# Down projections of a decoder trunk as one Strassen step, with weight sums built in device memory

## The reference

```
def swiglu(x, w_gu, w_down):
    g, u = jnp.split(x @ w_gu, 2, axis=-1)
    return (jax.nn.silu(g) * u) @ w_down
...
    for l in range(DEPTH):
        x = layer_norm(ALPHA * x + 0.5 * swiglu(x, ffn1_w_gu[l], ffn1_w_down[l]), ln_w[l, 0], ln_b[l, 0])
        mix = hybrid_mixer(x, positions, w_in[l], b_in[l], attn_sinks[l], mlstm_norm_w[l],
                           conv_w[l], w_branch[l], w_out[l])
        x = layer_norm(ALPHA * x + mix, ln_w[l, 1], ln_b[l, 1])
        x = layer_norm(ALPHA * x + 0.5 * swiglu(x, ffn2_w_gu[l], ffn2_w_down[l]), ln_w[l, 2], ln_b[l, 2])
```

## Time and profile before

| what | value |
|---|---|
| median of three runs | 2335.39 us |
| profiled execution: its own time | 2335.44 us |
| profiled execution: its span | 2333.7 us |
| PE busy, share of the span | 2319.9 us, 99% |
| DVE busy | 1565.4 us, 67% |
| ACT busy | 971.3 us, 42% |
| POOL busy | 19.0 us, 1% |
| mean DMA rate over the span | 106 GB/s |
| first down stage, 233.4 to about 353 us: DVE busy in its first 60 us | 28.02 us |
| gate and up stage, 33 to 133 us: DVE busy | 91.69 us |

### The profile page before, as it was taken

How to read it: one execution, slowest core, us unless ns; L and a number is a source line. 1 busy time by engine, 2 the same in 40 slices (tenths; PEclk the granted TensorE clock), 3 DMA queues, 4 the chain that set the end, 5 groups by cost and what they waited for, 6 DMA issues and landing times.

```text
span 2333.7 us, 34884 instructions
## 1 busy us (share of the span) xinstructions
PE 2319.9 (99%) x14416; PEld 2089.5 (90%) x14416; DVE 1565.4 (67%) x2262; ACT 971.3 (42%) x1497; POOL 19.0 (1%) x16
## 2 busy tenths in 40 slices
PE   8999999999999999999999999999999999999998
PEld 8999888888888899998899998898888888999987
DVE  8988446554654698883598883565455647988834
ACT  5444324434443354443254453233344433544531
POOL 0000300000000000000000000000000000000000
PEclk9999999999999999999999999999999999999999
DMA  5333434323233333333233333243233233333421
GB/s 166 106 101 118 141 104 136 95 73 96 94 95 108 127 91 109 108 110 109 90 92 109 109 109 108 88 152 97 73 95 99 83 117 114 104 102 99 131 104 72
DMA packets 295053, 247.08 MB, mean 106 GB/s; under 512 B 13136, under 2 KB 256880, under 8 KB 294896
## 3 DMA queue, kind: packets, MB, share of 16 engines
q1 hardware_dynamic: 294352, 244.34, 33.8%
q10 hardware_dynamic: 544, 0.52, 0.1%
HBM read 238.51 MB, written 6.31 MB: 105 GB/s over the span
## 4 chain that ended last, share of the span: by engine, by line
PE 99%; DVE 0%; DMA 0%; DVEq 0%; ACT 0%; issue 0%
PE main L1585 10%; PE main L1587 10%; PE main L1586 10%; PE main L1741 6%; PE main L1739 6%; PE side L1740 6%; PE side L1739 6%; PE main L1740 6%; PE side L1741 6%; PE main L1691 5%; PE main L1693 5%; PE main L1692 5%; PE side L1691 4%; PE side L1692 4%; PE side L1693 4%; PE main L1674 1%
## 5 line engine op out<-in xcount | busy, mean ns | idle before, releaser
L991 DVE TENSOR_TENSOR wl<-raw,wh 128x1024 fp32r<-128x1024 f32 (+2 forms) x277 | 305.9, 1147 | 447.6 <-ACT wh L649 447.3
L649 ACT ACTIVATE wh<-raw 128x1024 fp32r<-128x1024 f32 (+2 forms) x277 | 260.8, 994 | 319.1 <-PE side L1693 175.2
L1585 PE MATMUL main<-xh,wh 128*128 128x512 f32 x848 | 334.4, 394 | 0.0
L1587 PE MATMUL main<-xl,wh 128*128 128x512 f32 x848 | 330.4, 390 | 0.0
L1586 PE MATMUL main<-xh,wl 128*128 128x512 f32 x848 | 330.2, 389 | 0.0
L1587 PEld LDWEIGHTS main<-xl,wh 128*128 128x128 f32 x848 | 159.2, 188 | 33.7
L1585 PEld LDWEIGHTS main<-xh,wh 128*128 128x128 f32 x848 | 159.2, 188 | 33.2 <-issue 0.3
L736 ACT ACTIVATE wh<-tw 128x1024 fp32r<-128x1024 f32 x80 | 84.8, 1060 | 248.3 <-PE side L1741 117.4
L1586 PEld LDWEIGHTS main<-xh,wl 128*128 128x128 f32 x848 | 159.4, 188 | 31.7
L1739 PE MATMUL side<-sum_hi,wh 128*128 128x256 f32 x640 | 181.1, 283 | 0.0
L1740 PE MATMUL side<-sum_hi,wl 128*128 128x256 f32 x640 | 181.1, 283 | 0.0
(11 more groups left out here) (301 smaller groups left out, 5712.4 us busy)
## 6 DMA issues: line engine op xcount, KB each, us to landing
raw<-gu SPq DMA_DIRECT2D x326, 256.0 KB, 4.0
raw<-w_in SPq DMA_DIRECT2D x100, 512.0 KB, 4.6
raw<-down SPq DMA_DIRECT2D x80, 512.0 KB, 4.6
raw<-w_branch SPq DMA_DIRECT2D x24, 512.0 KB, 4.4
raw<-w_out SPq DMA_DIRECT2D x16, 512.0 KB, 4.4
raw<-w_in SPq DMA_DIRECT2D x28, 256.0 KB, 3.6
raw<-gu SPq DMA_DIRECT2D x13, 512.0 KB, 5.8
raw<-down SPq DMA_DIRECT2D x16, 256.0 KB, 2.7
```

The lines of the kernel that those rows point to most:

```text
L649: ins = act.activation(put(wh[block_of(g)]), get(raw[slot]), ACT.Copy)
L991: ins = V.tensor_tensor(put(wl[b]), get(raw[slot]), f32(put(wh[b])), ALU.subtract)
L1585: T.matmul(out, hi, rh(k), start=k == 0, stop=False)
L1587: ins = T.matmul(out, hi, rl(k), start=False, stop=k == kk - 1)
```

## The change

The hidden activations A (512 by 2816) and the down weight W (2816 by 1024) are each cut in two by two blocks: A by tokens (256 each) and by hidden chunks (11 each, `KH`), W by hidden chunks and by output columns (512 each). Seven block products replace eight. They run one after the other, each over all its 11 chunks, in the order P1, P5, P6, P3, P2, P7, P4. `DOWN` lists the 22 slabs of this: three slabs (4, 4 and 3 chunks) for each product, four (4, 3, 2 and 2) for P4. A product has two token tiles, so it takes 11 x 2 x 3 = 66 matmuls.

- The token operands are `hp` itself for P1, P2 and P4, and sums made by DVE (`operand_sum`) for the others, in `sf` (laid over `xh`) or in place in `hp`. ACT and DVE split each into `ah` and `al`, one buffer of four for each slab.
- The weight operands of P5, P6, P7 and P4 are the sums T1 to T4 of blocks of W. They lie in device memory (`tsum`). POOL builds them with DMAs: for each sum and each quarter of its rows first a copy (`begin`) and then a DMA that adds onto it, 32 DMAs of 352 rows by 512 columns (0.72 MB) for each of the four down stages. They are started when `w_lo` reaches 8, the first 32 before `angles`, the other 96 after it. SP waits for a sum (`blocks_summed`) before it loads its first slab.
- The results go from PSUM into `xt` product by product (`residual`), where P6, P7 and P4 collect on top of P1 in the same two banks, and P3 on top of P5. A product that reuses a bank waits in PE until DVE has read it (`part_used`).
- The order of the tails is written anew: tiles 0 and 1 are complete after P2 and are normalised by DVE while it prepares P4's first two slabs, tiles 2 and 3 after P4. The load of `xt` in the first block moves from the down stage to the gate and up stage (`c == 12`).

```diff
-S_FFN = KF + 12
+KH = KF // 2
+P1, P5, P6, P3, P2, P7, P4 = range(7)
+DOWN = tuple((r, k, n) for r in range(6) for k, n in ((0, 4), (4, 4), (8, 3))) + tuple((P4, k, n) for k, n in ((0, 4), (4, 3), (7, 2), (9, 2)))
+ENDS = tuple(max(j for j, d in enumerate(DOWN) if d[0] == r) for r in range(7))
+SUMMED = tuple(j for j, d in enumerate(DOWN) if d[0] in (P5, P6, P3, P7))
+T1, T2, T3, T4 = range(4)
+TURNED_BLOCKS = {P5: T1, P6: T2, P7: T3, P4: T4}
+PARTS = 4
+PART = KH * P // PARTS
+S_FFN = KF + len(DOWN)
...
+        sf = at("sf", [P, KH, 256], F32, xh_at)
...
+        ah = [big(f"ah{i}", kb, [P, 4, 256], F32R) for i, kb in enumerate((60, 44, 52, 76.25))]
+        al = [big(f"al{i}", kb + 4, [P, 4, 256], F32R) for i, kb in enumerate((60, 44, 52, 76.25))]
...
+        tsum = [nc.dram_tensor(f"tsum{i}", (4, KH * P, HALF), F32, kind="Internal").ap() for i in range(2 * DEPTH)]
...
+                return (r_, p_, q_)[(n - KF) % 3]
...
+                    if c == 12 and layer + f == 0:
+                        for t in range(NB):
+                            sp.dma_start(xt[:, t, :], token_tile(x_in, t)).then_inc(xt_in[t].sem, 16)
+                for j, (r, k0, kk) in enumerate(DOWN):
+                    if r in TURNED_BLOCKS:
+                        if k0 == 0:
+                            for i in range(PARTS):
+                                sp.wait_ge(blocks_summed[i].sem, 16 * (8 * u + 2 * TURNED_BLOCKS[r] + 2))
+                        src = tsum[u][TURNED_BLOCKS[r]].rearrange("(k p) n -> p k n", p=P)[:, k0:k0 + kk, :]
+                    else:
+                        low_rows, right = {P1: (0, 0), P2: (KH, 0), P3: (KH, HALF)}[r]
+                        src = wd[:, low_rows + k0:low_rows + k0 + kk, right:right + HALF]
+                    load(n0 + KF + j, src)
+                    if j == 4:
+                        sp.wait_ge(hid_f.sem, hid_f.val(layer, 22 * f + 22))
+                        rows(layer, 2 * f)
+                        if layer == 0 and f == 0:
+                            sp.dma_start(positions_in[:, :], positions[0, :].partition_broadcast(P)).then_inc(pos_in.sem, 16)
...
-            def hidden_high(layer, f, c):
-                act.wait_ge(hid_f.sem, hid_f.val(layer, 22 * f + c + 1))
-                act.activation(hh[c][:, :], hp[:, c, :], ACT.Copy).then_inc(*o.up(hid_h))
+            def operand_high(layer, f, j):
...
+                if j == 0:
+                    act.wait_ge(w_lo.sem, 2 * (n0 + KF))
+                else:
+                    act.wait_ge(slab_done.sem, n0 + KF + max(0, j - 3))
+                if j in SUMMED:
+                    act.wait_ge(tokens_summed.sem, len(SUMMED) * (2 * layer + f) + SUMMED.index(j) + 1)
+                else:
+                    act.wait_ge(hid_f.sem, hid_f.val(layer, 22 * f + (k0 + kk if r == P1 else KF)))
+                act.activation(ah[j % 4][:, 0:kk, :], operand(j), ACT.Copy).then_inc(*o.up(part_hi))
...
+                for j in range(2, len(DOWN)):
+                    split(n0 + KF + j)
+                    operand_high(layer, f, j)
+                    if layer == 0 and f == 0 and j == 14:
...
+                    if j == 17:
+                        root(L, 0)
+                    if j == 18:
+                        root(L, 1)
...
+            def sum_blocks_of(layer, f):
...
+                for t in (T1, T2, T3, T4):
+                    for i, t_, out_, begin, add in steps:
+                        if t_ == t:
+                            if 8 * u + 2 * t:
+                                pool.wait_ge(blocks_summed[i].sem, 16 * (8 * u + 2 * t))
+                            G.dma_start(out_, begin).then_inc(blocks_summed[i].sem, 16)
+                    for i, t_, out_, begin, add in steps:
+                        if t_ == t:
+                            pool.wait_ge(blocks_summed[i].sem, 16 * (8 * u + 2 * t + 1))
+                            G.dma_start(out_, add, accum_op=ALU.add).then_inc(blocks_summed[i].sem, 16)
+            pool.wait_ge(w_lo.sem, 8)
+            sum_blocks_of(0, 0)
             angles()
+            for layer, f in ((0, 1), (1, 0), (1, 1)):
+                sum_blocks_of(layer, f)
...
-            def hidden_low(layer, f, c):
-                dve.wait_ge(hid_h.sem, hid_h.val(layer, 22 * f + c + 1))
-                V.tensor_tensor(hl[:, c, :], hp[:, c, :], f32(hh[c][:, :]), ALU.subtract).then_inc(*o.up(hid_l))
+            def operand_sum(layer, f, j):
...
+                a11, a21 = hp[:, k0:k0 + kk, 0:256], hp[:, k0:k0 + kk, 256:512]
+                a12, a22 = hp[:, KH + k0:KH + k0 + kk, 0:256], hp[:, KH + k0:KH + k0 + kk, 256:512]
+                held = sf[:, k0:k0 + kk, :]
+                if r == P5:
+                    dve.wait_ge(slab_done.sem, n0 + KF)
+                    dve.wait_ge(hid_f.sem, hid_f.val(layer, 22 * f + KF))
+                    out_, a, b, op = held, a21, a22, ALU.subtract
+                elif r == P6:
+                    dve.wait_ge(part_lo.sem, len(DOWN) * u + j - 2)
+                    out_, a, b, op = held, held, a11, ALU.subtract
+                elif r == P3:
+                    dve.wait_ge(part_lo.sem, len(DOWN) * u + j - 2)
+                    out_, a, b, op = held, a12, held, ALU.add
+                else:
+                    dve.wait_ge(tokens_summed.sem, len(SUMMED) * u + 3)
+                    out_, a, b, op = a21, a11, a21, ALU.subtract
+                V.tensor_tensor(out_, a, b, op).then_inc(*o.up(tokens_summed))
+            def operand_low(layer, f, j):
+                u, kk = 2 * layer + f, DOWN[j][2]
+                dve.wait_ge(part_hi.sem, len(DOWN) * u + j + 1)
+                V.tensor_tensor(al[j % 4][:, 0:kk, :], operand(j), f32(ah[j % 4][:, 0:kk, :]), ALU.subtract).then_inc(*o.up(part_lo))
...
+            def residual(layer, f, r):
...
+                for i in range(2):
+                    if i == 0:
+                        dve.wait_ge(part_done.sem, norm_parts(L) + r + 1)
+                    else:
+                        dve.wait_ge(slab_done.sem, n0 + KF + ENDS[r] + 1)
+                    t = i if r in (P1, P6, P3, P2) else 2 + i
+                    p = 1 if r in (P5, P6, P3, P7) else 0
+                    some = xt[:, t, HALF * p:HALF * p + HALF]
+                    ps = pm[2 + i][:, :] if r in (P1, P6, P7, P4) else sd[:, i, :] if r in (P5, P3) else pm[i][:, :]
+                    told = part_used if r != P4 else acc_free if i else None
+                    if r in (P1, P5, P6, P4):
+                        if L == 0 and r in (P1, P5):
+                            dve.wait_ge(xt_in[t].sem, 16)
+                        V.scalar_tensor_tensor(out=some, in0=some, scalar=ALPHA, in1=ps, op0=ALU.mult,
+                                               op1=ALU.subtract if r == P6 else ALU.add).then_inc(*o.up(told))
+                    else:
+                        dve.wait_ge(part_used.sem, 12 * u + 2 * {P3: P6, P2: P1, P7: P5}[r] + i + 1)
+                        V.scalar_tensor_tensor(out=some, in0=ps, scalar=-1.0 if r == P7 else 1.0, in1=some, op0=ALU.mult,
+                                               op1=ALU.add).then_inc(*o.up(told))
+                    if r in (P3, P2, P7, P4):
+                        o.settle()
+                        V.bn_stats(lst[:, t, p, :], some).then_inc(*o.up())
+                    if r in (P2, P4):
+                        o.settle()
+                        apart(dve)
+                        V.bn_aggr(lag[:, t, :], lst[:, t, :, :]).then_inc(*o.up(var_ready))
+                    if r == P4:
+                        scale(L, t)
+                        finish(L, t)
+                        if i == 0 and L < NORMS - 1:
+                            split(n0 + S_FFN + 1)
...
+                for j in range(2, len(DOWN)):
+                    if j in SUMMED:
+                        operand_sum(layer, f, j)
+                    split(n0 + KF + j)
+                    operand_low(layer, f, j)
+                    if j - 2 in ENDS:
+                        residual(layer, f, ENDS.index(j - 2))
+                    if j in (17, 18):
+                        if j == 17:
+                            dve.wait_ge(rows_in_.sem, 32 * (L + 1))
+                        scale(L, j - 17)
+                        finish(L, j - 17)
+                if L < NORMS - 1:
+                    low(L + 1, 0)
+                    low(L + 1, 1)
+                    split(n0 + S_FFN)
+                residual(layer, f, P4)
+                if L < NORMS - 1:
+                    low(L + 1, 2)
+                    if in_sums(n0 + S_FFN + 2):
+                        sums_13(n0 + S_FFN + 2)
+                    low(L + 1, 3)
...
-                pe.wait_ge(hid_f.sem, hid_f.val(layer, 22 * f + KF - 1))
-                to_tokens(3 * layer + 2 * f, n0 + KF, GROUPS_FFN, lambda k: hh[k], lambda k: hl[:, k, :],
-                          lambda k: pe.wait_ge(hid_l.sem, hid_l.val(layer, 22 * f + k + 1)))
...
+                def bank(r, i):
```

(103 more changed lines are left out.)

92 lines of the change are left out of this document (43 added, 49 removed).

## The result

Four runs after the change gave 2348.25 to 2355.91 us, median 2354.36, against 2335.31 before (2335.05 to 2335.64): ratio 1.0078, interval 1.0065 to 1.009. The kernel is 19 us slower. I had forecast 2310 and faster. The profiled execution took 2355.91, with a span of 2354.1.

A forecast was written before the change was run, and what follows sets the result against it. PE, busy 99% of the span, was taken to bound the kernel. 2335.4 - 59.9 (matmuls) + 16 (DVE idling) + 6 (hand-overs) + 12 (new DMAs and POOL's arithmetic) = 2309.5, say 2310; range 2286 to 2362.

The forecast's parts named there:

- PE's matmuls, -59.9: Down stages: 462 matmuls of the same shape, 0.2267 us apart, saving 15.0 us a stage, 59.9 in all.
- DVE's list, +16: Down stages: DVE's list equals PE's, so its idling delays P4's first matmul; 4 us a stage, 16 in all (0 to 36).
- Hand-overs, `xt` and POOL's arithmetic, +6, +2 and +5: Late tiles at stage ends 6 us; `xt`'s load in gate and up 2; DVE slowed beside the angles, first stage, 5.
- the bare saving: Whole kernel: the time before less only the removed matmuls, 2335.4 - 59.9, with no costs added.
- The adding DMAs, t = 5: POOL's sum DMAs: 5 us each (2.9 to 12.1), 160 us for a stage's 32, T1 complete near 90, hidden.
- That cover holds unless the landing doubles. I put 5 us: Gate and up stage: SP's loads, 9.5 us ahead and landing in some 4, lose 5 us to the DMAs (0 to 50).
- 1, DVE keeps up: Down stages: raw slabs land in time and DVE's list has no hole; 2287 us; chance 0.20.
- 2: First down stage: slow adding DMAs make ACT wait 32t - 237 for the angles, 2361 at t = 9; chance 0.14.
- its companion from the Trainium skill: DVE's two-port modes starve GpSimd's DMAs, so adds would crawl; by inference two-input subtraction does not, adding nothing.
- 3, the loads starve: Gate and up stage: loads queue behind 2 KB pieces, some 8 slabs pay 6 or 7 us; about 2355; chance 0.12.
- 4, DVE idles twice as much: Down stages: DVE idles 9 us a stage or more through handshakes and landings; 2330, nearly no gain; chance 0.14.
- The page's formula: POOL's DMAs: 2.0 us and bytes over 436 GB/s, 3.65 us for 0.72 MB, 117 us for 32 end to end.

The follow-up runs named there:

- e1: The changed kernel without POOL's sum DMAs; P5, P6, P7 and P4 read a plain block of the down weight, sums left out; 2309.28 us.
- e5: e1 with P7's update read out of PSUM ahead of slab 19's low parts, as in e3; 2283.61 us.
- e2: The changed kernel with `tsum`'s rows padded by 64 bytes, so copies from sum to sum move as 2 KB rows, not 45 KB pieces; 2333.85 us.
- e3: The changed kernel with P7 read out of PSUM right after slab 18's low parts, before slab 19's and tile 1's normalising; 2328.63 us.
- e4: The changed kernel with both the padded rows of e2 and the early reading of P7 of e3; 2309.62 us.
- e10: e7 without the padding of the sums' rows, so copies from sum to sum are again 45 KB pieces, one DMA in flight; 2299.93 us.
- e7: e4 with each of POOL's 128 DMAs issued only when the one before has landed; 2301.94 us.
- e6: e4 with POOL issuing the 96 DMAs of the later blocks' sums only when the first down stage is over; 2295.99 us.
- e11: e6 with one POOL DMA in flight, except T4's four adds, which wait only for their own copy; angles between T4's copies and adds; 2294.64 us.

## Why the prediction was wrong, point by point

- **PE's matmuls, -59.9: right.** In the second stage P1's first starts at 1086.70 and P7's last at 1176.26, 396 of them 0.2267 apart.
- **DVE's list, +16: right in place and cause, too small.** I had 88.0 us of work and 4 of idling; the window from 1088 to 1181 has 87.2 of DVE busy, and its waits for ACT there sum to 5.1. The gap is 4.6 to 5.0 where 4 was put. What I left out is the slow clock after it. Wait and clock together are 6.4 a stage by e1 and e5, 25.7 in all where 16 were put. The windows of the changed kernel:

```profile
1088.00:1181.00 93.00, 88.65 (x392) 73.06 (x390) 87.22 (x93) 55.32 (x64) 0.00 (x0) 0.99 0.59 193
```

- **Hand-overs, `xt` and POOL's arithmetic, +6, +2 and +5: too large together.** e5 has these and nothing else, and stands 2283.6 - 2275.5 = 8.1 above the bare saving, 13 less 4.9. That DVE slows by a quarter to a third beside the angles holds (1590 against 1223 ns).
- **The adding DMAs, t = 5: the price in sequence about right, each one dearer.** 32 of them took 180 us (45.8 to 226.2), 5.6 each, and SP hardly waited for a sum. But one lands in 8.2 and not in 5, and T1 was complete at 97.6, not near 90. My ground, "the four quarters overlap", holds for the copies only, two at a time in 2 KB pieces and four in long ones.
- **The step that failed: "That cover holds unless the landing doubles. I put 5 us".** The term measured 45.1 (e1). The landing of `raw<-gu` between 50 and 240 went from 3.9 (e1) to 6.8 in the middle, and at the bursts to over 16. It was also priced for the gate and up stage alone. The loads of the first down stage and of the mixer beside the same DMAs were put at nothing, and 16.5 and 11.2 of the 45 were lost there. I set the mean DMA share, 37%, against the mean cover, and took a DMA from device memory to itself to be made of 2 KB pieces strung out by waits. What decides is what stands in front of a load at one moment: three or four copies of 45 KB pieces. Of the 45.1 us the bursts are about 20: 20.5 from the changed kernel to e2 and 19.0 from e3 to e4, which differ in the padding alone. (e3 to e10 is 28.7, but its waits act on all of POOL's DMAs, and with short pieces the same waits gained 7.7, e4 to e7.) The next sums beside the first down stage, where loads are wanted soonest, are 13.6 (e4 to e6), and 12.4 stay (e6 to e5), whose place no run isolates. With so few runs, which spread by up to 20 us, these sizes are good to a few us.
- **The rivals.** 1, DVE keeps up (2287), is what e5 shows once the order is mended and the DMAs are gone: 2283.6. 2 did not come (SP and ACT did not wait for sums or angles), but e7 brought it about, at the price of its formula. Of its companion from the Trainium skill ("SBUF — State Buffer", "SBUF: two separate sides") the inference was the half that fits, that a two-input subtraction on DVE does not starve GpSimd's DMAs: with DVE 81% busy (46 to 226) POOL's "issue" waits are 7.3 us on average (138.8 in 19), and with DVE 57% busy (300 to 852) they are 7.4 (439.2 in 59). No run here shows the other half. 3, the loads starve, was the nearest: its sign (`tw<-raw` waits for `raw<-gu`, 19.3 us between 40 and 240) was there, and its 2355 is the time measured, which lies inside the range only through the prices of rivals 2 and 3. The agreement is in part luck. It had all its 50 us in the gate and up stage, eight slabs paying 6 or 7 each, where only two gaps of 6 stand and 17.8 were lost, and the errors of the other terms partly cancel, to 4.8. 0.12 was too little for it. 4, DVE idles twice as much: the list cost 25.7, midway between the sum's 16 and this rival's 36.
- **The page's formula** (the Trainium skill, "DMA: Bandwidth & Descriptors", "Anatomy of one DMA — SWDGE (gpsimd) path"), by which I estimated 3.65 us: too low here. One at a time beside SP's loads, the first 32 landed after 6.3 us on average for a copy (4.5 to 8.2) and 8.3 for an add (7.0 to 11.8) in e10.

## What to carry to other kernels

A DMA off the critical path is priced by what it puts in front of the loads that are on it, at its worst moment and not by the mean share: look how many of them can be issued in a row, and in how long pieces they move. Before a new wait on PE, lay out the list of the engine that ends it and put the awaited instruction first; here that was worth 25.7 us, more than the 18.9 us of the waits themselves, because PE's clock falls after a gap. The change pays once both are mended: e11 and e6 take 2294.6 and 2296.0 against 2335.3 before and 2354.4 as made, and 2283.6, which leaves the sums out, bounds what sums made at no cost would give.

## What the runs showed of the hardware

- A DMA of POOL that adds in device memory did not go out while another of its DMAs in 2 KB pieces was in flight, though no semaphore held it (56 of 64 in the changed kernel, all 64 in e6; the other 8 had only copies in 45 KB pieces in flight). Of the copies in 2 KB pieces no more than two were ever in flight; the third went out 0.3 us after the first had landed. Copies in 45 KB pieces went out 0.5 us apart, with an add still in flight, and four of them were in flight at once. So POOL's adds followed each other at least 7.3 us apart, with a median of 9.3. Why POOL waits for the landing was not found.
- PE's granted clock was 0.50 (1.2 GHz) after each of the changed kernel's eight gaps of 3.6 to 16.5 us, for 3 to 6 us. It also fell after shorter ones, of 2.5 (e6, 259.7: 0.57 in the 4 us after it) and 2.2 (e3, 832.2: 0.59). It stayed 1.00 after gaps of 2.5 (e6, 141.9), 2.8 (e10, 332.9), 2.9 (e11, 337.8) and 3.7 (e10, 268.3). So between 2.2 and 3.7 us the length of the gap alone doesn't decide.
